# Order of work inside the interleaved gate and attention steps of a decoder layer

## What is computed

```python
def project_inputs(x, pos, w_in):
    h = jnp.einsum('bsd,de->bse', x, w_in)
    qa, ka, va, qb, kb, vb, ga, gb = jnp.split(h, _col_splits(), axis=-1)
    ...
    return qa, ka, va, qb, kb, vb, jax.nn.sigmoid(ga), jax.nn.sigmoid(gb)

def _softmax_stats(scores, sink):
    lse = jax.nn.logsumexp(scores, axis=-1, keepdims=True)
    if sink is not None:
        lse = jnp.logaddexp(lse, sink)
    return jnp.exp(scores - lse), lse[..., 0]

def finish_layer(x, o_a, o_b, ga, gb, ...):
    br_a = jnp.einsum('bse,ed->bsd', o_a.reshape(N, S, A_Q_W), w_branch_a)
    br_b = jnp.einsum('bse,ed->bsd', o_b, w_branch_b)
    mix = jnp.einsum('bsd,de->bse', ga * br_a + gb * br_b, w_out)
    h = layer_norm(ALPHA * x + mix, ln1_g, ln1_b)
    u = jnp.square(jax.nn.relu(jnp.einsum('bsd,df->bsf', h, w_ff1) + b_ff1))
    f = jnp.einsum('bsf,fd->bsd', u, w_ff2) + b_ff2
    return layer_norm(ALPHA * h + f, ln2_g, ln2_b)
```

## Time and profile before

| | us |
|---|---|
| median of 3 runs | 1947.64 (1946.57 to 1947.89) |
| profiled execution, its own time | 1947.87 |
| its span, first to last instruction | 1946.3 |
| PE busy in the span | 1844.0 (95%) |
| DVE busy | 907.0 (47%) |
| ACT busy | 773.8 (40%) |
| stretch with interleaved attention, 379.9 to 762.9 | 383.0 |
| PE busy in that stretch | 342.6 |

### The profile page before, as it was taken

The page is one execution under the profiler, slowest core; times in us unless marked ns, Lnnn a source line. Parts: engine busy times, 40 slices in busy tenths (PEclk is TensorE's granted clock), DMA queues, the critical chain, the costliest instruction groups (busy, mean ns, idle before and its releaser), DMA issues.

```text
span 1946.3 us, 33735 instructions
## 1 busy us (share of the span) xinstructions
PE 1844.0 (95%) x12750; PEld 1776.2 (91%) x12750; DVE 907.0 (47%) x1197; ACT 773.8 (40%) x1063; POOL 102.3 (5%) x208
## 2 busy tenths in 40 slices
PE   8999999988898889999959999999999999999993
PEld 8999999977777778999949999999999999999992
DVE  5455443444444444664484443444344443444444
ACT  5454543444444445333344333333233432334322
POOL 0000000111110111100000000000000000000000
PEclk9999999999999999999969999999999999999996
DMA  7555555755555555665517666666666666666631
GB/s 251 152 150 147 172 168 162 256 194 207 180 193 176 187 184 183 204 196 172 169 38 256 207 215 218 210 225 203 213 206 233 203 216 203 235 207 215 213 110 54
DMA packets 270910, 369.04 MB, mean 190 GB/s; under 512 B 11920, under 2 KB 264528, under 8 KB 267904
## 3 DMA queue, kind: packets, MB, share of 16 engines
q1 hardware_dynamic: 250368, 249.17, 41.9%
q0 software_dynamic: 9088, 106.90, 14.4%
q10 hardware_dynamic: 11392, 12.13, 1.8%
HBM read 356.02 MB, written 70.71 MB: 219 GB/s over the span
## 4 chain that ended last, share of the span: by engine, by line
PE 84%; DVE 8%; ACT 5%; issue 2%; DMA 0%; ACTq 0%; DVEq 0%; SPq 0%
PE psM L964 26%; PE psM L965 26%; PE psM L966 26%; DVE s_wlo L672 2%; ACT s_whi L419 2%; ACT L553 1%; DVE s_st L774 1%; PE psO L1072 1%; PE psM L1012 1%; ACT s_S L500 1%; PE psO L1059 1%; DVE s_S L758 1%; DVE s_r L889 1%; DVE s_r L898 1%; PE psT L1038 0%
## 5 line engine op out<-in xcount | busy, mean ns | idle before, releaser
L672 DVE TENSOR_TENSOR s_wlo<-s_raw,s_whi 128x1024 fp32r<-128x1024 f32 x468 | 573.2, 1226 | 916.5 <-ACT s_whi L419 911.6
L419 ACT ACTIVATE s_whi<-s_raw 128x1024 fp32r<-128x1024 f32 x468 | 495.0, 1058 | 834.4 <-PE psM L966 815.8
L964 PE MATMUL psM<-s_xhi,s_whi 128*128 128x320 f32 x1248 | 396.8, 318 | 21.1 <-ACT s_gstage L553 11.5
L965 PE MATMUL psM<-s_xlo,s_whi 128*128 128x320 f32 x1248 | 390.5, 313 | 0.0
L966 PE MATMUL psM<-s_xhi,s_wlo 128*128 128x320 f32 x1248 | 390.4, 313 | 0.0
L964 PE MATMUL psM<-s_hhi,s_whi 128*128 128x320 f32 x1024 | 317.9, 310 | 8.9 <-DVE s_hlo L884 8.6
L965 PE MATMUL psM<-s_hlo,s_whi 128*128 128x320 f32 x1024 | 317.5, 310 | 0.0
L966 PE MATMUL psM<-s_hhi,s_wlo 128*128 128x320 f32 x1024 | 317.5, 310 | 0.0
L964 PE MATMUL psM<-s_uhi,s_whi 128*128 128x320 f32 x1024 | 316.4, 309 | 0.0
L965 PE MATMUL psM<-s_ulo,s_whi 128*128 128x320 f32 x1024 | 316.4, 309 | 0.0
L966 PE MATMUL psM<-s_uhi,s_wlo 128*128 128x320 f32 x1024 | 316.4, 309 | 0.0
(11 more groups left out here) (160 smaller groups left out, 1636.5 us busy)
## 6 DMA issues: line engine op xcount, KB each, us to landing
s_raw<-in_w_ff_dram SPq DMA_DIRECT2D x256, 512.0 KB, 3.6
s_raw<-in_w_in_dram SPq DMA_DIRECT2D x156, 512.0 KB, 3.9
s_kvbuf<-in_kT_b_dram POOLq DMA_DIRECT2D x8, 2448.0 KB, 8.6
s_kvbuf<-in_v_b_dram POOLq DMA_DIRECT2D x8, 2304.0 KB, 8.4
s_raw<-in_w_out_dram SPq DMA_DIRECT2D x32, 512.0 KB, 3.5
out_b_s_dram<-in_cache_b_kv_dram POOLq DMA_DIRECT2D x16, 1008.0 KB, 6.0
s_raw<-in_w_branch_a_dram SPq DMA_DIRECT2D x16, 512.0 KB, 3.5
gates_scratch<-s_gstage ACTq DMA_DIRECT2D x16, 320.0 KB, 4.0
```

The source lines that it names most:

```text
L419: act.activation(whi[:, slot], raw[:, slot], ACT.Copy).then_inc(hi_done, 1)
L672: dve.tensor_tensor(wlo[:, slot], raw[:, slot], whi[:, slot].bitcast(F32), ALU.subtract).then_inc(lo_done, 1)
L964: pe.matmul(out, wh, hi[:, t0 + k], start=first and k == 0, stop=False)
L965: pe.matmul(out, wh, lo[:, t0 + k], start=False, stop=False)
```

## The change

`gate`, `between` and `attend` of each engine become one function `step(n, k, at)`, so that the order inside a step can mix them. TensorE's instructions keep their order. On ScalarE a step is now: where k = 0, `sigmoids(n - 1)`; the split; where k = 0, the store of the gates (`store_gates`, a function of its own now); the evictions and `turned_probs` of units s - 2 to s; and last `exps` of unit s + 2. On VectorE a step is now: `back` of unit s + 1, `front` of unit s + 2, the split, then `stage`. Both calls on VectorE and the one on ScalarE are so one unit further on, and they start at step -2. No computation, buffer, DMA or semaphore is added or removed.

```diff
-        def gates_and_attention(gate, between, attend, end):
-
-            for n in range(2):
+        def gates_and_attention(step, end):
+
+            for n in range(NGATE - 1):
                 for k in range(4):
-                    gate(n, k)
-                between(n)
-            for n in range(2, NGATE - 1):
-                for k in range(4):
-                    if n > 2 or k >= 2:
-                        attend(at(4 * (n - 3) + k))
-                    gate(n, k)
+                    s = 4 * (n - 3) + k
+                    step(n, k, at(s) if s >= -2 else None)
...
                 act.activation(gstage[:, n % 2], gate_bank(n)[:, :, 0:NTOK], ACT.Sigmoid).then_inc(gate_evac, 1)
+
+            def store_gates(n):
                 act.wait_ge(gate_evac, n + 1)
                 act.dma_start(gates_d[2 * n:2 * n + 2].rearrange("t p n -> p t n"), gstage[:, n % 2]
                               ).then_inc(gate_stored[n % 2], 16)
 
-            def gate(n, k):
+            def step(n, k, at):
 
                 if n < 2 or n == NGATE - 1:
                     split(G_G + n + 1, k)
-                elif k > 0:
+                    if n == 0 and k == 3:
+                        sigmoids(0)
+                        store_gates(0)
+                        turn_out(G_G - 1, 0, G_G - 1, "v")
+                    return
+                if k == 0:
+                    sigmoids(n - 1)
+                if k > 0:
                     split(G_G + n + 1, k - 1)
                 elif n > 2:
                     split(G_G + n, 3)
-                else:
-                    sigmoids(1)
...
-            def attend(at):
-                s = at(0)
-                if at(1):
-                    exps(*at(1))
-                if s and s[2] % 4 == 0:
-                    sigmoids(s[2] // 4 + 2)
+                if k == 0:
+                    store_gates(n - 1)
+                if at is None:
+                    return
                 if at(-2) and UNITS[at(-2)[1]][0] == "SB":
                     o_evac(*at(-2))
                 if at(-1):
                     (sums_evac if UNITS[at(-1)[1]][0] == "SB" else o_evac)(*at(-1))
-                if s:
-                    turned_probs(*s)
+                if at(0):
+                    turned_probs(*at(0))
+                if at(2):
+                    exps(*at(2))
 
             def end():
+                sigmoids(NGATE - 2)
                 split(G_BR - 1, 3)
-                sigmoids(NGATE - 2)
+                store_gates(NGATE - 2)
...
-            def gate(n, k):
+            def step(n, k, at):
 
                 if n < 2 or n == NGATE - 1:
                     split(G_G + n + 1, k)
-                elif k > 0:
+                    if n == 1 and k == 3:
+                        stage_first()
+                    return
+                if at is not None:
+                    if at(1):
+                        back(*at(1))
+                    if at(2):
+                        front(*at(2))
+                if k > 0:
                     split(G_G + n + 1, k - 1)
                 elif n > 2:
                     split(G_G + n, 3)
-
-            def between(n):
-                if n == 1:
-                    stage_first()
-
-            def attend(at):
-                if at(0):
-                    back(*at(0))
-                if at(1):
-                    front(*at(1))
-                if at(0) and at(4) and UNITS[at(4)[1]][0] in ("SB", "SA"):
+                if at is not None and at(4) and UNITS[at(4)[1]][0] in ("SB", "SA"):
                     stage(*at(4))
...
```

More of the change, by code:

```diff
@@ L219, in at @@
             return one
-        def gates_and_attention(gate, between, attend, end):
-            for n in range(2):
+        def gates_and_attention(step, end):
+            for n in range(NGATE - 1):
                 for k in range(4):
-                    gate(n, k)
-                between(n)
-            for n in range(2, NGATE - 1):
-                for k in range(4):
-                    if n > 2 or k >= 2:
-                        attend(at(4 * (n - 3) + k))
-                    gate(n, k)
+                    s = 4 * (n - 3) + k
+                    step(n, k, at(s) if s >= -2 else None)
             end()
             for k in range(4):
-                gate(NGATE - 1, k)
+                step(NGATE - 1, k, None)
         def wait(eng, s, value):
@@ L565, in gate @@
                     split(G_G + n, 3)
-                else:
-                    sigmoids(1)
-            def between(n):
-                if n == 0:
-                    sigmoids(0)
-                    turn_out(G_G - 1, 0, G_G - 1, "v")
-            def attend(at):
-                s = at(0)
-                if at(1):
-                    exps(*at(1))
-                if s and s[2] % 4 == 0:
-                    sigmoids(s[2] // 4 + 2)
+                if k == 0:
+                    store_gates(n - 1)
+                if at is None:
+                    return
                 if at(-2) and UNITS[at(-2)[1]][0] == "SB":
@@ L594, in end @@
                     act.activation(ohi[:, 4 * j:4 * j + 4], oT[:, 4 * j:4 * j + 4], ACT.Copy).then_inc(o_hi, 1)
-            gates_and_attention(gate, between, attend, end)
+            gates_and_attention(step, end)
             sigmoids(NGATE - 1)
+            store_gates(NGATE - 1)
             with act.Fori(0, 2) as i:
@@ L1089, in turn_sums, with step @@
                 mm.then_inc(pv, 1)
-            def gate(n, k):
+            def step(n, k, at):
+                if at is not None:
+                    if at(2):
+                        if at(2)[2] == 0:
+                            pe.wait_ge(gate_evac, 2)
+                        unit_scores(*at(2))
+                    if at(-2) and UNITS[at(-2)[1]][0] == "SB":
+                        turn_sums(*at(-2))
+                    if at(-1):
+                        unit_values(*at(-1))
+                    if at(0):
+                        if at(0)[2] == 0:
+                            pe.wait_ge(turned_out, 13)
+                        turn_probs(*at(0))
                 if k == 0 and n == 0:
```

## The result

The changed kernel takes 1890.41 us (1890.34 to 1891.25, 4 runs) against 1947.77 us: the ratio is 0.9707, with a 95% interval of 0.969 to 0.9723. That is 57 us less, where 48.8 were forecast; the time lies 1.6 us under the low end of the range. The direction and the place of the gain were right, and the forecast gain was too small by 8 us.

A forecast was written before the change was run, and what follows sets the result against it. The prediction took TensorE's gaps and clock as the bound, its waits coming from ScalarE's and VectorE's order. Waits 42.4 us plus clock 6.4 us make 48.8 us off the 1947.64 us median: 1898.8 us, range 1892 to 1916 us.

The forecast's parts named there:

- What bounds the kernel: Interleaved attention stretch: TensorE idle 40.4 us of 383.0, its waits all ending on the order of work in ScalarE or VectorE.
- the L1021 row under "issue": 8.7 us of TensorE waits listed as issue; claimed to be SB scores waiting behind the mask of an A unit.
- The order on VectorE: `front` ahead of the split: mask ends about 1 us after its scores, `masked` waits go; a later split half costs nothing.
- The order on ScalarE: Split, about 1.06 us, ahead of the evictions, hidden in most steps; sigmoid first where k = 0, its waits gone except s = 0.
- The cost of a wait: 49 TensorE waits: 40.3 us listed plus 0.07 each makes 43.7 us, less 1.3 at s = 0: 42.4 us.
- The clock: Five stretch chunks partly at 1.2 GHz lose 9.4 us; one or two slow ones expected to remain (3 us), so 6.4 return.
- Rival 1: Clock does not come back, slow chunks standing behind small matmuls, which stay: gain 42.4 us, 1905.2 us; chance 0.15.
- Rival 2: Sigmoid stays late on ScalarE if table switches cost twice 1.28 us: seven waits, 7.7 us, 1906.5 us; chance 0.07.
- Rival 3: New waits on VectorE (`exped`) and ScalarE (`shifted`) take half: gain 26.6 us, 1921.0 us; chance 0.09.
- Rival 4: Cached keys and values come too late, with 4.3 us of slack left: slower, up to 1966 us; chance 0.04.
- Rival 5: Change does nothing: another dependency fills the same TensorE gaps, 1947.6 us; chance 0.03.
- The range: Whole kernel time: 1892 us at the low end to 1916 us at the high end, reaching part of rival 3.

## Why the prediction fell short

**What bounds the kernel**: right. The seven rows of waits, put down to the order on ScalarE and VectorE, were the gain; the L1021 row under "issue" vanished with the others when `front` alone was moved, so it was a wait for the mask too.

**The order on VectorE**: right, and more than was said. `front` ahead of the split is the whole effect. The late second half of the split cost nothing, as reckoned: VectorE waits 97 us for it in one of the runs with no loss. The sign that VectorE's split should no longer wait for ScalarE's came nearly: three such waits of 9.9 us in all are left in the stretch, where there were 51 of 204.8 us.

**The order on ScalarE**: right that the split is hidden, but its moved place is worth nothing once VectorE's order is new. The text also said that the sigmoid "now stands first"; its place against `exps` is what it was, and it came early because `exps` did. It matters only that it was not put behind the split or the evictions.

**The cost of a wait: the step that failed.** The prediction took 0.07 us on top of each listed idle time, from one pair of starts that both had 64-row scores. From before to after the gaps ahead of the scores shrank by 33.2 us for 28.8 us listed, and those ahead of the chunks, with the attention between them, by 14.1 us for 10.8 listed (11.5 less the 0.7 that stay): 47.4 us, where 42.4 were forecast. The listed idle time begins when a matmul has ended, but where nothing waits the next one starts before that, and how long before differs from place to place. Scores with 128 rows start 0.15 us after the last matmul and not 0.24. A chunk starts 0.03 us after the last transposition has started, where with a wait listed as 1.30 us it started 1.58 us after it. The surplus is 0.16 us a wait, and not 0.07. That is 4.4 us of the miss, and 0.6 us more came from s = 0, where 0.7 us were left and not 1.3.

**The clock: the second failed term.** 6.4 us were forecast, 9.4 came back in the chunks. The 3 us held back were one or two spells that were to remain, and the prediction gave no reason for them: by its own count of waits all 9.4 us were to come back, since the changed kernel was to have no wait of the kind left. The count itself, three falls of three with waits on both sides, did not hold either. It left out four steps of the kernel before (s = 4, 16, 28 and 40) with 0.20 us ahead of the scores and 1.30 us ahead of the chunk, and full clock; and the runs with waits on one side had slow spells too. 5.0 + 3.0 us is the miss of 8.0 us in the stretch, which by its starts became 56.8 us shorter.

**Rival 1** (small matmuls alone hold the clock down) fell: there was no slow spell in 48 steps that all end in transposes. It is the rival that the prediction's sentence on the page means, though it says "the second". The Trainium skill's rule that transposes do not count as busy ("TensorE: Matmul & The Clock Gate", Part 4: PE-mode transpose) did not by itself bring the clock down here; whether transposes help a wait to do so, no run here shows. **Rival 2** fell by the trace after: the table load runs ahead of the sigmoid's wait (466.86, sigmoid at 468.92), and no drain shows. **Rival 3** did not come. **Rival 4** did not come, but it was nearer than it looked. For the sequence that was read the earlier trace rows the forecast of 4.3 us was good: 4.2 were left. It did not stand for the others. In before the slacks of the seven were 6.1 to 11.4 us, and they lost 2.2 to 9.9 us, not 2.9 each, since the time from issue to scores was 18.4 to 21.9 us and is 15.3 in all seven. Some loads also took longer (8.7 to 9.7 us from issue to landing, against 8.5 to 8.8); the higher DMA share (0.65 against 0.56) goes with that, but no run shows that it is the cause. **Rival 5** did not come.

**The range** was too narrow below: its low end took the waits at 42.4 us and all of the clock, and beyond that 4 us that also had to hold the 5.0 us by which the waits were underpriced, from a single reading.

## What to carry to other kernels

In an engine's list, put what another engine waits for next ahead of what is needed some steps later, even if the latter is ready first: `front` moved ahead of the split on VectorE was worth 57 us, and the rest of the reordering nothing more (alone, ScalarE's part would have been worth 54). When several kinds of wait sit in one loop, look for a single lateness that passes through all of them before pricing them apart. Price a removed wait by the start-to-start gap against a place without a wait of the same operation, and count the clock with it: the 40.3 us listed here, less the 0.7 that stay, were worth 56.8.

## What the hardware showed unexpectedly

- With waits on one side of small matmuls the clock fell too, 12 times of 12 behind a late sigmoid's waits of 2.5 us and more; it did not fall in 48 steps of small matmuls and transposes with one wait of 0.7 us, nor with 0.16 us more ahead of each of 48 scores.
- A table load of ScalarE runs before the semaphore wait of the activation that needs it: load from 466.86 to 468.14, sigmoid at 468.92.
- A wait of TensorE for its own matmul just before is not free: it put the scores at 0.37 us after that matmul's start instead of 0.24 or 0.15, and cost 7.7 us ahead of 48 scores, none of which the list of waits shows.
